# Second attention: GpSimd scales the probabilities head by head, and VectorE copies a turned bank in every step from the fifth on

## What is computed

```python
def softmax_attend(q, k, v):
    s = jnp.einsum('bkgqd,bkld->bkgql', q, k).astype(jnp.float32) * (q.shape[-1] ** -0.5)
    p = jax.nn.softmax(s, axis=-1).astype(v.dtype)
    return jnp.einsum('bkgql,bkld->bkgqd', p, v)
...
    k_all = jnp.concatenate([kc, kl], axis=2)
    v_all = jnp.concatenate([vc, vl], axis=2)
    ol = merge_heads(blocked_attend(ql, k_all, v_all)) @ w_o
```

## Time and profile before

| what | value |
|---|---|
| median of three runs | 1506.48 us (1505.92 to 1506.79) |
| profiled execution, first to last instruction | 1505.7 us |
| TensorE busy | 1428.6 us |
| VectorE busy | 952.1 us |
| ScalarE busy | 612.7 us |
| GpSimd busy | 392.8 us |
| second attention, first turn to first product of `wo` | 1228.67 to 1283.34 us of the span |

### The profile page before, as it was taken

One profiled execution on the slowest core, in us unless ns is written; L12 is line 12 of the kernel. 1 busy time (PEld: TensorE's weight loads), 2 busy tenths in 40 slices (PEclk: granted clock), 3 DMA queues, 4 the chain that ended last, 5 costly groups with the idle time before them and its releaser, 6 DMA issues.

```text
span 1505.7 us, 24502 instructions
## 1 busy us (share of the span) xinstructions
PE 1428.6 (95%) x10534; PEld 1239.9 (82%) x10534; DVE 952.1 (63%) x1132; ACT 612.7 (41%) x729; POOL 392.8 (26%) x302
## 2 busy tenths in 40 slices
PE   5899999979999999998899999999999998899999
PEld 5888899979999996763577888888886965899999
DVE  6888765566768666858738777255415578586333
ACT  5623445343344364533623322322223447433433
POOL 4975703000004400000002343442320010034553
PEclk9999999999999999999999999999999999999999
DMA  7542334556676565853536654344333400465552
GB/s 249 170 141 85 113 111 139 186 181 203 217 237 224 172 220 180 234 176 85 175 102 210 193 179 156 126 145 149 121 102 113 168 29 2 140 224 171 193 170 82
DMA packets 156084, 236.15 MB, mean 157 GB/s; under 512 B 6577, under 2 KB 126417, under 8 KB 155857
## 3 DMA queue, kind: packets, MB, share of 16 engines
q1 hardware_dynamic: 152336, 230.78, 46.5%
q10 hardware_dynamic: 3648, 3.92, 1.1%
HBM read 227.55 MB, written 1.05 MB: 152 GB/s over the span
## 4 chain that ended last, share of the span: by engine, by line
PE 82%; DVE 8%; POOL 5%; ACT 3%; issue 2%; DMA 1%; DVEq 0%; SPq 0%; ACTq 0%; POOLq 0%
PE bank L2119 24%; PE bank L2120 23%; PE bank L2121 23%; PE bank L2429 2%; DVE wlo L1163 1%; PE bank L2183 1%; POOL X L1973 1%; PE bank L2597 1%; PE bank L2586 1%; PE bank L617 1%; PE bank L2262 1%; DVE stat L1858 1%; PE bank L2308 1%; DMA A<-in_w_mod 1%; PE bank L2271 1%
## 5 line engine op out<-in xcount | busy, mean ns | idle before, releaser
L2119 PE MATMUL bank<-ahi,whi 128*128 128x256 f32 (+1 forms) x2480 | 792.4, 320 | 23.7 <-DVE alo L1630 4.9
L2120 PE MATMUL bank<-alo,whi 128*128 128x256 f32 (+1 forms) x2480 | 782.5, 316 | 0.0
L2121 PE MATMUL bank<-ahi,wlo 128*128 128x256 f32 (+1 forms) x2480 | 782.1, 315 | 0.0
L1163 DVE TENSOR_TENSOR wlo<-raw,whi 128x2048 fp32r<-128x2048 f32 x160 | 367.5, 2297 | 357.2 <-ACT whi L689 356.8
L689 ACT ACTIVATE whi<-raw 128x2048 fp32r<-128x2048 f32 x160 | 306.3, 1914 | 658.6 <-PE bank L2121 658.5
L2119 PEld LDWEIGHTS bank<-ahi,whi 128*128 128x128 f32 x2480 | 476.4, 192 | 71.4 <-issue 26.6
L2121 PEld LDWEIGHTS bank<-ahi,wlo 128*128 128x128 f32 x2480 | 476.6, 192 | 28.7
L2120 PEld LDWEIGHTS bank<-alo,whi 128*128 128x128 f32 x2480 | 476.8, 192 | 26.9 <-issue 0.2
L2086 POOL TENSOR_TENSOR A<-A 128x512 f32 (+1 forms) x48 | 106.8, 2238 | 480.0 <-ACT A L1029 480.0
L2068 POOL TENSOR_TENSOR alo<-A,ahi 128x512 fp32r<-128x512 f32 (+1 forms) x43 | 126.5, 2945 | 354.3 <-ACT ahi L895 354.3
L1524 DVE SCALAR_TENSOR_TENSOR A<-modraw,scc,A 128x1024 f32<-128x1024 f32 x70 | 121.3, 1772 | 0.6
(11 more groups left out here) (306 smaller groups left out, 1219.6 us busy)
## 6 DMA issues: line engine op xcount, KB each, us to landing
raw<-in_w_ff SPq DMA_DIRECT2D x64, 1024.0 KB, 5.2
modraw<-in_w_mod SPq DMA_DIRECT2D x72, 512.0 KB, 4.6
raw<-in_w_in SPq DMA_DIRECT2D x28, 1024.0 KB, 5.1
A<-in_w_mod SPq DMA_DIRECT2D x24, 512.0 KB, 5.3
raw<-in_pw SPq DMA_DIRECT2D x12, 1024.0 KB, 6.6
raw<-in_w_ffn_gate SPq DMA_DIRECT2D x11, 1024.0 KB, 5.3
raw<-in_w_ffn_up SPq DMA_DIRECT2D x11, 1024.0 KB, 5.4
raw<-in_w_ffn_down SPq DMA_DIRECT2D x11, 1024.0 KB, 5.1
```

What stands on the lines that cost most here:

```text
L1163: dve.tensor_tensor(wlo[:, k % 2, :], raw[:, (k + 2) % 4, :], whi[:, k % 2, :].bitcast(F32), ALU.subtract).then_inc(wlo_ready, 1)
L2119: pe.matmul(out_, w_hi, a_hi, start=start, stop=False, **kw)
L2120: pe.matmul(out_, w_hi, a_lo, start=False, stop=False, **kw)
L2121: return pe.matmul(out_, w_lo, a_hi, start=False, stop=stop, **kw)
```

## The change

The two multiplications of each step go from VectorE to GpSimd. VectorE still takes the reciprocals, now into one of three pairs of columns of `stat` (`reciprocals(i)`), and signals `gden_ready`. GpSimd scales one head after the other and signals `pn_ready` after each; `gturn` waits for each head by itself, just before the four transposes of that head. `copied_on_dve` holds for every step from i = 4 on, not only the even ones. On VectorE the reciprocals now stand ahead of the bank copy. On GpSimd the first step's scaling stands between `cosine_part(4)` and `cosine_part(5)`, the others behind the latter. Three semaphores that nobody waited for are dropped.

```diff
         def copied_on_dve(i):
-            return i >= 4 and i % 2 == 0
+            return i >= 4
+
+        def reciprocals(i):
+            return stat[:, 52 + 2 * (i % 3):54 + 2 * (i % 3)]
...
-            def gscale(i):
-                s0, s1 = 20 + 2 * (i % 3), 36 + 2 * (i % 2)
+            def gden(i):
+                s0 = 20 + 2 * (i % 3)
                 dve.wait_ge(exp_done, TR + 2 * (i + 1))
-                link(dve.reciprocal(stat[:, s1:s1 + 2], stat[:, s0:s0 + 2]))
-                for b in range(2):
-                    m = dve.tensor_scalar(pg[:, i % 3, b, :], pg[:, i % 3, b, :], stat[:, s1 + b:s1 + b + 1],
-                                          None, ALU.mult)
-                m.then_inc(pn_ready, 1)
+                dve.reciprocal(reciprocals(i), stat[:, s0:s0 + 2]).then_inc(gden_ready, 1)
...
+                if 0 <= i - 2 < GSTEPS:
+                    gden(i - 2)
                 if i - 3 < GSTEPS and copied_on_dve(i - 3):
                     gptb(i - 3)
-                if 0 <= i - 2 < GSTEPS:
-                    gscale(i - 2)
...
             pool.wait_ge(gtab_landed, 16)
-            for e in range(6):
+            def gscale(i):
+                pool.wait_ge(gden_ready, i + 1)
+                for b in range(2):
+                    pool.tensor_scalar(pg[:, i % 3, b, :], pg[:, i % 3, b, :], reciprocals(i)[:, b:b + 1],
+                                       None, ALU.mult).then_inc(pn_ready, 1)
+
+            for e in range(5):
                 cosine_part(e)
+            gscale(0)
+            cosine_part(5)
+            for i in range(1, GSTEPS):
+                gscale(i)
...
             def gturn(i):
-                pe.wait_ge(pn_ready, TR + i + 1)
                 if i >= 1:
                     pe.wait_ge(pt_ready, TR + 2 * i)
                 for b in range(2):
+                    pe.wait_ge(pn_ready, TR + 2 * i + b + 1)
```

More of the change, by code:

```diff
@@ L269, in program @@
         scc_ready = sem("scc_ready")
-        silu_ready = sem("silu_ready")
         sin_in = sem("sin_in")
         sin_out = sem("sin_out")
-        rtab_ready = sem("rtab_ready")
         tab_ready = sem("tab_ready")
@@ L314, in program @@
         hlo_ready = sem("hidden_lo_ready")
-        x_ready = sem("x_ready")
         phi_ready = sem("p_hi_ready")
@@ L359, in program @@
         gq_ready = sem("gq_ready")
+        gden_ready = sem("second_attention_reciprocals")
         block = ctx.enter_context(nc.Block())
@@ L1252, in _ @@
             dve.wait_ge(scc_ready, 1)
-            dve.tensor_tensor(scc[:, 0:16], scc[:, 0:16], C["cc"], ALU.mult).then_inc(silu_ready, 1)
+            dve.tensor_tensor(scc[:, 0:16], scc[:, 0:16], C["cc"], ALU.mult)
             dve.wait_ge(pos_landed, 16)
```

## The result

| | before | changed |
|---|---|---|
| median of 4 runs | 1506.63 us (1505.92 to 1511.82) | 1527.36 us (1525.91 to 1532.19) |
| ratio | | 1.0133, 95% interval 1.0113 to 1.0153 |
| span of the profiled execution | 1505.7 us | 1525.6 us |
| first scores of the second attention to first product of `wo` | 64.55 us | 83.41 us |

The account below looks back on a forecast made before the run. TensorE was taken as the bound in the steady middle, waiting for scaling at the head, in places and at the end. -0.95 up to weigh 13 and +0.72 at the end gave about -0.2: 1506.3 us, range 1504.4 to 1510.2.

Parts of the forecast that it names:

- What the scaling costs on either engine: Second attention's scaling: VectorE's pair 0.88 us; GpSimd taken at 0.60 us a head, from the one-input row L2057.
- From above: the two-input L2101, 1.26 us: Upper bound on GpSimd's scaling of one head, taken from a two-input row: 1.26 us.
- GpSimd is too slow: Rival: scaling over 0.67 us a head delays odd steps; times 1508 to 1516; chance 0.17 for over 0.8.
- steeper then: Within the slow-GpSimd rival: beyond 0.92 us a head the loss grows faster than before, about +10 us at 1.26.
- About 0.15 us earlier per turn: Wherever TensorE really waits for scaling, the turn starts about 0.15 us earlier, 0.24 if only head 0 counts.
- the head: Start of the second attention: turn 0 about 0.3 us earlier, turn 1 by 0.15 to 0.2; step 1 gains 0.2.
- -0.95 up to weigh 13: Gains at the head and in the middle together bring weigh 13 about 0.95 us earlier.
- The waits that "stay": Middle: TensorE's waits of 0.44 and 1.60 us end longer chains that remain; each shrinks only by 0.15 to 0.24.
- The end, +0.72: Step 15's bank copy, now on VectorE behind the 2.28 us wlo block, makes weigh 13 to wo 0.72 us longer.
- The added 0.8 for what lies around the span: Forecast span 1505.5 us raised to a time of 1506.3, the span being 0.8 short of the median before.
- falls at the end: Rival: TensorE idles 1.7 us before weigh 15, 0.94 before wo; its clock falls, costing up to 1.7 us; chance 0.15.
- The two rules of the skill: Port exclusion holds nothing at 0.60 us a head; GpSimd level with VectorE for one input, twice as slow for two.

Follow-up runs that it names:

- at 1.488: Changed kernel with GpSimd multiplying by the constant 0.5 instead of the column of reciprocals: 1523.82 us, ratio 1.0108.
- With the reciprocals ahead: Changed kernel with VectorE taking a step's reciprocals ahead of the next step's reductions instead of behind them: 1517.09 us, ratio 1.0066.
- with two operations: Changed kernel with GpSimd's instruction also adding the constant 0 after multiplying by the column: 1509.9 us, ratio 1.0014.
- the two-input run: Changed kernel with GpSimd multiplying two tensors, the reciprocal column spread over 512 columns as the second: 1513.95 us, ratio 1.0045.
- the two price lists: Kernel before plus GpSimd operations on spare SBUF behind the last cosine_part, 57 in one list, 42 in the other; total times say nothing.

## Why the prediction was wrong

**The step that failed** is the price in "What the scaling costs on either engine": "I take 0.60: it has one streamed input, so it is nearest to L2057". A head takes 1.563. The row was read rightly: 0.49 us behind the held start, with the 0.1 for an opening, fits the 0.618 measured for that form. But L2057 multiplies and adds, the change's instruction only multiplies, and the page prints both as TENSOR_SCALAR, 128x512 from 128x512. I matched rows by name and shape and did not compare the source lines, where the second operation stands. The one difference that I saw, the column of scalars, is worth 0.075. "From above: the two-input L2101, 1.26 us" failed too: it was no bound, the slow one-input form lies over it. So the range ended at 1510.2, and the time is 1527.4.

**The rival "GpSimd is too slow"** had the mechanism and nearly the slope. It had +3 us at 0.92 and "about +10" at 1.26. The runs: +1.2 in the stretch at 0.692, +6.4 at 1.041, +16.5 at 1.488, +18.9 at 1.563. On straight lines between these, 0.92 gives +4.6 and 1.26 gives +11.3. That its times ended at 1516, and its chance of 0.17 beside 0.52, came from the price alone. (The steps that it calls odd are those of even number: the turn at 1255.66 is that of step 8, and the torn turns of the changed kernel are of such steps.)

**What "steeper then" meant** I had not worked out. From turn 0 to turn 15 the changed kernel takes 66.94 us, 50.37 before, 16.6 more. The pair of steps without a clock drop takes 8.08 and not 6.22: 1.86 for each of seven pairs, 13.0. The three further stretches at half clock add 1.12, 1.15 and 0.88 to their pair or step. Turn 0 itself comes 0.74 later behind the first scores, and from turn 15 to `wo` it is 1.55 longer. Together 18.4 of the 18.9. With the reciprocals ahead, a pair takes 7.3, 1.1 over the floor and not 1.86, so the ring makes about 0.75 of each pair, beside what it does to the clock. That ring was not in the prediction: it followed the scaling into TensorE, and not from there back into VectorE's queue.

**"About 0.15 us earlier per turn" and the head.** Turn 0 was to come 0.3 earlier. With 1.563 the wait ahead of it is 3.40 against 2.65. With 0.692 the wait is 2.53; the head by head signal on VectorE alone makes it 2.25. So the small gain at the head is the signal's, and moving the scaling to GpSimd adds nothing to it.

**The middle, and -0.95 up to weigh 13.** No run has a head at 0.60; the nearest is 0.692, with two operations. There weigh 13 comes 58.90 us behind the first scores, 58.40 before: 0.50 later and not 0.95 earlier. Turns mostly stand 3.11 to 3.25 apart, but the six of even number from 4 to 14 take 1.20 to 1.24 us and not 1.09, together 0.8: head 1 comes late into each. The slow rival, counting from 0.67, gives 0.05 a step at this price; it is 0.11 to 0.15. The waits that "stay" stayed: the 1.60 ahead of the turn of step 10 is 1.71 with two operations. Of the bank copies only the last is late, as written, and that they are hidden only because the scaling left VectorE was right as well: alone they cost 3.8 us in the stretch.

**The end, +0.72.** Right in place, sign and size. With two operations the last copy stands straight behind `wlo`, weigh 15 waits 1.69 for it, inside the 1.5 to 2 forecast, and from weigh 13 (1282.06) to `wo` (1288.93) it is 6.87 us, 6.15 before. In the changed kernel the wait is 1.06. Its VectorE:

```profile
1297.11 2.28 DVE L1164 TENSOR_TENSOR wlo<-raw,whi 128x2048 fp32r<-128x2048 f32 x1
1299.31 0.68 DVE L1871 COPY A<-bank 128x512 f32<-128x512 f32 x1
```

Giving that one copy back to ScalarE brings more than 0.72, since the earlier turn 15 then counts: 1.35 us of the stretch at 1.49 a head and 1.49 us at 0.69.

**The sum as a whole.** With the price at 0.692 the stretch is 1.2 us longer, 0.50 and 0.72, where the sum had -0.95 and 0.72. The end was the sound half of it. The added 0.8 for what lies around the span was low: the changed kernel's profiled execution took 1527.41 beside a span of 1525.6, 1.8, as in every run below.

**The clock.** In the changed kernel there were three more drops, behind torn turns all through the attention, and none at the end: weigh 15 waited 1.06 us, `wo` 0.94, and TensorE stayed at full clock. But the rival "falls at the end" was drawn for a wait of 1.7 us, and with the quick form, which has it, the clock did fall as `wo` began. The rival had up to 1.7 us for it; that execution is 2.5 us longer behind the stretch. So the mechanism to which the prediction gave 0.15 is real where its condition is met. The condition is not the length of the waits alone: in the two-input run, with 1.70 and 0.94, the clock stayed at 1.00 (1288.0 to 1300.0).

**The two rules of the skill.** L1861, the small product on which the exponentials hang, was held by scalings in flight (columns as in the rows of one line above, then VectorE in order of time):

```profile
L1861 DVE TENSOR_SCALAR stat<-stat x16: 168/170/525, 1221.2 to 1290.2; 128x2 f32<-128x2 f32 x16
```

```profile
1255.01 0.16 DVE L1866 RECIPROCAL stat<-stat 128x2 f32<-128x2 f32 x1
...
1258.04 0.35 DVE L1861 TENSOR_SCALAR stat<-stat 128x2 f32<-128x2 f32 x1
...
1274.94 0.53 DVE L1861 TENSOR_SCALAR stat<-stat 128x2 f32<-128x2 f32 x1
```

170 ns in most steps, up to 525 while GpSimd scaled; with 0.692 a head up to 274. The Trainium skill, SBUF — State Buffer, "Who interferes with whom", has a VectorE instruction in a two-port mode and one of GpSimd take the shared ports by turns, each for a whole instruction. The trace agrees in part. Of seven L1861 that started beside a head of GpSimd four ended as that head ended, as the one at 1258.04 (the head of the chain above ends at 1258.38). One was not held at all, and two ended in the middle of a head, as the one at 1274.94, whose head runs to 1276.32. The prediction had the hold only from 0.9 a head on; the 274 ns stand at 0.692. The six holds add up to 1.2 us; how much of it reached TensorE no run shows. The Trainium skill, GPSIMD Engine Reference, "Engine selection", has GpSimd about twice as slow as VectorE for two inputs and roughly level with it for one. The first half is near: 1.26 us against 0.69 for a VectorE instruction of two such tensors (L1838 at 1226.84 before), 1.8 times. The second is wrong for the change's instruction, 1.563 against 0.44 for half of VectorE's pair, 3.5 times, and nearer for the one with two operations, 0.692, 1.6 times. Its advice to keep elementwise work on VectorE was a better guide than its figure for one input.

**Left open.** How the half clock and the ring share the 9.0 us that came back behind turn 2 with the reciprocals moved; what besides the waits decides whether the clock falls; and why a single operation is slow on GpSimd, of which the runs show only that it is.

## What to carry to other kernels

A row prices an added instruction only if it has the same operations in the same slots as well as the same engine, shape and operands: read the source line of the row, not its name. Where no row has that form, an upper bound from another form is none, and the rival behind it should be priced until it stops being linear. When work moves to another engine, follow its output round until it comes back to that engine's input; if the way leads through a queue in which later work stands ahead, as the reciprocals behind the next reductions here, a slow engine is also starved.

## What the runs showed of the hardware

On GpSimd, float32, 128 partitions, in place, with the other engines at work on the kernel, the shortest of three (from the two price lists):

| form | 128 columns | 512 columns |
|---|---|---|
| copy | 0.289 us | 0.613 us |
| constant, one operation | 0.527 us | 1.488 us |
| column of scalars, one operation | 0.602 us | 1.563 us |
| constant, two operations | 0.302 us | 0.626 us |
| column and constant, two operations | 0.373 us | 0.695 us |
| column spread as a second tensor | 0.399 us | 1.039 us |

One operation costs 2.5 ns a column, two cost 0.84, as the copy does; a second tensor 1.67. A column of scalars adds about 0.07 us to an instruction, at 128 columns as at 512. So a product by a column, with 0 added in the same instruction, takes 0.692 us in the kernel where the bare product takes 1.563.

TensorE's clock: torn turns, of a kind that the kernel before does not have, were followed by 3.4 us at 1.2 GHz in three places of the changed kernel, where TensorE had waited 1.13, 2.58 or 1.71 us and then 0.82, and in the others, where it had waited 0.18 to 0.65 and then 0.82, by none. Time lost to a wait was there paid a second time, about 1.1 us for each such stretch. Waits of 1.7 and 0.94 us ahead of `wo` were followed by 6.8 us at 1.2 GHz in the run with two operations and by none in that with two inputs.
